# A fused two-block transformer kernel: order of the first weight load, low half, operand halves and copies

## The chip, the cores and the metric

The kernel runs on one core of one Trainium2 chip. The metric is the device time of one execution in microseconds. It computes in fp32 accuracy by splitting each operand of a matrix product into a high half, rounded to the format fp32r, and a low half, the remainder.

## The reference

The reference is a chain of three transformer layers on 256 tokens of width 1024: a first block with two layers, conditioned on a vector `c`, and a second block with one. The change touches only the start of the first layer:

```python
cond = jax.nn.silu(c)
mod = (cond @ ada_w[i] + ada_b[i])[:, None, :]
shift1, scale1, gate1, shift2, scale2, gate2 = jnp.split(mod, 6, axis=-1)
h = rmsnorm(x, norm1_g[i]) * (1.0 + scale1) + shift1
qkv = h @ w_qkv            # 1024 x 3072 in the first layer
```

So the product with `w_qkv` can't begin before `cond @ ada_w` is known for shift and scale, which are 2048 columns of 1024 rows, 8 MB. The rest of the kernel is attention, the feed-forward parts and the second block, in the same manner of computing.

## The kernel before

The program is written for each engine by hand; engines wait on each other's semaphores (`wait_ge`), and each engine and each queue works in program order.

*Weights.* All weights pass in tiles of 512 KB, numbered through the whole kernel. SyncE loads tile m to one of 4 buffers `raw`, after `low(m - 4)` has freed it (`slot_free`). ScalarE makes the high half `w_hi` (`split(m)`, line 638), VectorE the low half `w_lo` (`low(m)`, line 1156), which raises `lo_done`. TensorE waits for `lo_done` m + 1 and does 12 matmuls of 512 columns (`wide`, lines 1900 to 1902): for two token halves and two rows of blocks, high x high, high x low, low x high. There are 6 buffers of `w_hi` and `w_lo`, and a split waits for the tile 6 ahead of it to be done (`SPL`). Tiles 0 to 23 are the QKV projection (`TILES_A` orders them as column chunk and quarter u of the contraction: tiles 0 to 5 take quarters 0 and 1, tiles 6 to 11 quarters 2 and 3).

*Modulation.* `ada_w` comes in pieces of 512 KB too (`load_ada(a)`), all on SyncE's queue: c, pieces 0 and 1, x, pieces 2 to 8, weight tiles 0 to 3, pieces 9 to 13, then tiles and pieces by turns. VectorE multiplies each by its element of `cond` and adds it up (`fold(a)`, line 1186, the first of a sum at line 1183). Eight folds make a vector, spread over 128 partitions; 16 pieces make two vectors, half 0 and half 1 of shift and scale together. `reduce_vector` on TensorE adds over the partitions by 16 one-column matmuls (line 2025): the first before tile 0, the second behind tile 4, and it waits for `fold(15)`. Then `modulate(h)` on VectorE makes `mod` and `gains` for its half, and for its two quarters kk the modulated operand: VectorE writes `hf_mod` (line 1339) from the normed and transposed x (`hf`), ScalarE writes the high half `h_hi` directly from `hf` (`high_0`, line 770, two instructions a quarter), and VectorE subtracts, which gives `h_lo` (line 1344) and raises `h_lo_ok`. Each tile waits for its quarter's `h_lo_ok`, quarter u as `h_lo_ok` u + 1.

*Order on VectorE:* folds 0 to 8, modulation of half 0 with `low(0)` inside it, behind its first `h_lo`; `low(1)`, `low(2)`, folds 9 and 10, `low(3)`, folds 11 and 12, `low(4)`, folds 13 to 15, `low(5)`, `low(6)` (written `low(SPL)`), modulation of half 1, and from then on a low half and now and then a fold (`low(QKV_A + SPL + m)`), with tables for the attention between them. *Order on ScalarE:* `split(0)`, `high_0` of quarters 0 and 1, splits 1 to 7, `high_0` of quarters 2 and 3, then split 8 and so on with the evacuation of finished chunks between. Attention scores begin behind tile 20.

Of the kernel before, what the change touches and what calls it, by code (L numbers as in the profile page):

```python
# [11 lines left out]
ALU = mybir.AluOpType  # L12
ACT = mybir.ActivationFunctionType
AX = mybir.AxisListType

P = 128
D = 1024
S = 256
T = S // P
# [16 lines left out]
QKV_A, WO_A, IN_0, OUT_0, QKV_B, WO_B, IN_1, OUT_1 = 0, 24, 32, 76, 98, 110, 118, 162  # L36
# [9 lines left out]
TILES_A = [(c, u) for u0 in (0, 2) for c in range(3) for u in (u0, u0 + 1)] + [(c, u) for c in range(3, 6) for u in range(4)]  # L46
BANKS_A = (0, 1, 2, 1, 0, 1)
# [90 lines left out]
def program(nc, x_in, c_in, ada_w, ada_b, norm1_g, norm2_g, a_w_qkv, a_w_o, lq1, lk1, lq2, lk2,  # L138
# [4 lines left out]
    with ctx:  # L143
        def sem(name):
            return ctx.enter_context(nc.semaphore(name))
# [7 lines left out]
        w_hi = sb("w_hi", [P, SPL, 2, CH], F32R)  # L153
        w_lo = sb("w_lo", [P, SPL, 2, CH], F32R)
        h_hi = sb("h_hi", [P, KD, S], F32R)
        h_lo = sb("h_lo", [P, KD, S], F32R)
# [6 lines left out]
        mod = sb("mod", [P, 8 * VECTORS])  # L163
        gains = sb("gains", [P, KD])
# [48 lines left out]
        hf = at_p("hf", [P, KD, S], 2048)  # L213
        hf_mod = at_p("hf_mod", [P, KD // 2, S], 4096)
# [28 lines left out]
        bank = [ctx.enter_context(nc.psum_tensor(f"bank{n}", [P, CH], F32)) for n in range(8)]  # L243
# [14 lines left out]
        lo_done = sem("lo_done")  # L258
        mm_done = sem("mm_done")
# [22 lines left out]
        raw_x = sem("raw_x")  # L282
        hf_ok = sem("hf_ok")
        h_hi_ok, h_lo_ok = sem("h_hi_ok"), sem("h_lo_ok")
        res_ok = sem("res_ok")
        x_ok = sem("x_ok")
        evac = sem("evac")
        gate_mm, gate_ok = sem("gate_mm"), sem("gate_ok")
        bias_zero, bias_in = sem("bias_zero"), sem("bias_in")
        s_act = sem("s_act")  # L290
# [49 lines left out]
        def _(sp):  # L340
# [50 lines left out]
                load_ada(a)  # L391
            for t in range(T):
                sp.dma_start(x[:, t], x_in[0, t * P:(t + 1) * P, :]).then_inc(x_load, 16)
            for a in range(2, 9):
                load_ada(a)
            for m in range(4):
                load_a(m)
            for a in range(9, 14):
                load_ada(a)
# [23 lines left out]
            for k in range(KF):  # L423
                if k + 8 < KF:
                    load_tall(OUT_0 + 8 + k, f_w_out[0], 8 + k)
                else:
                    m = k + 8 - KF
# [201 lines left out]
        def _(act):  # L629
# [135 lines left out]
            def high_0(kk):  # L765

                act.wait_ge(raw_x, kk + 1)
                act.wait_ge(gain_ok, kk // 2 + 1)
                for k in (2 * kk, 2 * kk + 1):
                    last = nc.scalar.activation(h_hi[:, k], hf[:, k], ACT.Identity, scale=gains[:, k:k + 1],  # L770
                                                bias=mod[:, k:k + 1])
                last.then_inc(h_hi_ok, 1)

            act.wait_ge(setup_t, 2)
            nc.scalar.activation(vecs[:], bank[1][:, 0:237], ACT.Copy).then_inc(setup, 1)
# [54 lines left out]
            for i in range(NH + 3):  # L830
                if 2 <= i < NH:
                    exp_a(i)
                if 2 <= i < NH + 2:
                    h = i - 2
# [7 lines left out]
                if i >= 3:  # L842
                    h = i - 3
# [153 lines left out]
            for t in range(T):  # L997
                last = nc.scalar.activation(proj[:, t, 0:1536], proj[:, t, 0:1536], ACT.Gelu)
# [3 lines left out]
            for t in range(T):  # L1002
                last = nc.scalar.activation(rope_tc[:].rearrange("p a b c -> p (a b c)"), proj[:, t, 768:1536], ACT.Square,
                                            accum_out=stat[:, SS + t:SS + t + 1])
# [135 lines left out]
        def _(v_):  # L1140
# [9 lines left out]
            def low(m, turn=None):  # L1150

                if m >= END:
                    return
                m = at(m, turn, LOOP)
                v_.wait_ge(hi_done, m + 1)
                ve.tensor_tensor(w_lo[:, m % SPL], raw[:, m % RAW], w_hi[:, m % SPL].bitcast(F32),  # L1156
                                 ALU.subtract).then_inc(lo_done, 1)
                if m in TAKE_AFTER:
                    take_vector(TAKE_AFTER[m])
                for a, q in FOLD_AFTER.items():  # L1160
                    if q == m:
                        fold(a)

            def fold(a):

                g, k = divmod(a, 8)
                tile, arrived, count = ada_tile(a)
                acc, w = acc_of(g), tile.rearrange("p a n -> p (a n)")
                v_.wait_ge(arrived, count)
                if k == 0:  # L1170
                    if g in SHARED_WITH:

                        v_.wait_ge(ada_red, COLUMN[SHARED_WITH[g]] + 1)
                    if g:

                        v_.wait_ge(ada_done, a)
                    if g in GATES:

                        v_.wait_ge(bias_in, 16 * (GATES.index(g) + 1))
                        ve.scalar_tensor_tensor(out=acc, in0=w, scalar=cond[:, 0:1], in1=acc, op0=ALU.mult,  # L1180
                                                op1=ALU.add).then_inc(ada_done, 1)
                    else:
                        ve.tensor_scalar(acc, w, cond[:, 0:1], None, ALU.mult).then_inc(ada_done, 1)
                else:
                    v_.wait_ge(ada_done, a)
                    last = ve.scalar_tensor_tensor(out=acc, in0=w, scalar=cond[:, k:k + 1], in1=acc, op0=ALU.mult, op1=ALU.add)  # L1186
                    if k < 7 or g not in BY_BLOCKS:
                        last.then_inc(ada_done, 1)
                    else:

                        link(last)
                        link(ve.transpose(w, acc))
                        v_.wait_ge(ada_red, COLUMN[g])
                        ve.tensor_reduce(block_sums[:], w.rearrange("p (b r) -> p b r", r=32), AX.X, ALU.add).then_inc(ada_done, 1)
# [130 lines left out]
            def modulate(h):  # L1325

                v_.wait_ge(ada_red, h + 1)
                part = lambda row, first: row[:, first:first + 16].rearrange("p (v h q) -> p h v q", v=2, h=2)[:, h]
                ve.tensor_tensor(part(mod, 0), sums_of(h).rearrange("p (v q) -> p v q", v=2), part(vecs, ADAB_V),
                                 ALU.add).then_inc(ada_col, 1)  # L1330
                v_.wait_ge(ada_col, h + 1)
                ve.scalar_tensor_tensor(out=gains[:, 4 * h:4 * h + 4], in0=mod[:, 8 + 4 * h:12 + 4 * h], scalar=1.0,
                                        in1=vecs[:, N1_V + 4 * h:N1_V + 4 * h + 4], op0=ALU.add,
                                        op1=ALU.mult).then_inc(gain_ok, 1)
                v_.wait_ge(gain_ok, h + 1)
                for kk in (2 * h, 2 * h + 1):
                    v_.wait_ge(raw_x, kk + 1)
                    for k in (2 * kk, 2 * kk + 1):
                        last = ve.tensor_scalar(hf_mod[:, k % 4], hf[:, k], gains[:, k:k + 1], mod[:, k:k + 1],
                                                ALU.mult, ALU.add)  # L1340
                    last.then_inc(hf_ok, 1)
                    v_.wait_ge(hf_ok, kk + 1)
                    v_.wait_ge(h_hi_ok, kk + 1)
                    ve.tensor_tensor(h_lo[:, 2 * kk:2 * kk + 2], hf_mod[:, 2 * kk % 4:2 * kk % 4 + 2],
                                     h_hi[:, 2 * kk:2 * kk + 2].bitcast(F32), ALU.subtract).then_inc(h_lo_ok, 1)
                    if kk == 0:
                        low(0)

            for a in range(8):
                fold(a)  # L1350
            fold(8)
            v_.wait_ge(setup, 2)
            modulate(0)
            low(1)
            low(2)
            fold(9)
# [5 lines left out]
            for a in range(13, 16):  # L1362
                fold(a)
            low(5)
            low(SPL)
            modulate(1)

            def minus_lambda():
                v_.wait_ge(side_in, 16 * SIDE)
# [513 lines left out]
        def _(pe):  # L1883
            mm = nc.tensor.matmul

            def wide(m, u, b, v, turn=None, wait_operand=False, wait_1=None):


                if wait_operand:
                    pe.wait_ge(h_lo_ok, 4 * OLD[v] + u + 1)  # L1890
                m = at(m, turn, LOOP)
                pe.wait_ge(lo_done, m + 1)
                s = m % SPL
                for t in range(T):
                    if t == 1 and wait_1 is not None:
                        pe.wait_ge(*wait_1)
                    o = bank[2 * b + t][:]
                    for k in range(2):
                        hi, lo = (h[:, 2 * u + k, t * P:(t + 1) * P] for h in (h_hi, h_lo))
                        mm(o, hi, w_hi[:, s, k], start=(u == 0 and k == 0), stop=False)  # L1900
                        mm(o, hi, w_lo[:, s, k], start=False, stop=False)  # L1901
                        last = mm(o, lo, w_hi[:, s, k], start=False, stop=(u == 3 and k == 1))  # L1902
                last.then_inc(mm_done, 1)
# [143 lines left out]
            nc.tensor.transpose(bank[1][:, ADAB_V:ADAB_V + 96], stage_v[0:96, 2, :], ident[0:96, 0:96]).then_inc(setup_t, 1)  # L2047
            reduce_vector(0)

            def tile_a(m):  # L2050

                c, u = TILES_A[m]
                wide(QKV_A + m, u, BANKS_A[c], 0, wait_operand=True)

            for m in range(8):
                if m == 4:
# [510 lines left out]
```

## Time and profile before

| | us |
|---|---|
| median of 3 runs | 1038.45 (1038.05 to 1038.98) |
| span of the profiled execution | 1033.8 |
| median less that span | 4.65 |

The page's first table, as busy time and share of the span: TensorE (PE) 986.3 us, 95%; VectorE (DVE) 740.2 us, 72%; ScalarE (ACT) 542.6 us, 52%; GpSimd (POOL) 68.4 us, 7%. The profiled execution has its own span and no separate time outside it is recorded, so its place against the median is the difference above. In the page's 40 slices of 25.8 us the first has TensorE at two tenths, and the granted clock is nine tenths or more everywhere but in that slice, where it is eight. Queues: the core's 16 DMA engines moved 219.89 MB, 213 GB/s over the span. A matmul's row gives its start and its duration; matmuls overlap, so it is their distance that counts. A row of another engine may carry in brackets how long the engine was idle before and what ended the wait.

### The profile page before, as it was taken

To read this page: it belongs to the slowest core of one execution; us is meant where nothing else is said; L and a number is where in the kernel's file an instruction comes from. 1 tells how busy PE (TensorE), PEld (TensorE's weight loads), DVE (VectorE), ACT (ScalarE), POOL (GpSimd) and SP (SyncE) were. 2 spreads that over 40 slices of the span, in tenths; PEclk is the share of its full clock that TensorE was granted. 3 is DMA by queue.
4 is the path that set the end of the run, shared out by engine and by line. 5 is a ranking of instruction groups with operands and counts; after the bars stand their busy time and mean duration, and the time that the engine had idled before them with its cause. 6 is when DMAs were issued, how large, how long until landed. Compare 5 with 4: busy or idle time off the path is not lost.

```text
span 1033.8 us, 13550 instructions
## 1 busy us (share of the span) xinstructions
PE 986.3 (95%) x5102; PEld 827.2 (80%) x5102; DVE 740.2 (72%) x1053; ACT 542.6 (52%) x875; POOL 68.4 (7%) x126
## 2 busy tenths in 40 slices
PE   2999799999999999999999999999999999999997
PEld 2887577888878787778888886888888779999986
DVE  5988888878877897887665447647753777777643
ACT  4466846544443485575444436575546474444442
POOL 2100222000000411010000002000000010000000
PEclk8999999999999999999999999999999999999999
DMA  9998167998889472449865553856444367656551
GB/s 339 371 371 285 39 204 230 344 321 295 273 304 359 162 250 101 143 127 321 263 203 186 183 184 108 269 160 205 134 142 143 119 190 218 187 177 189 184 184 41
DMA packets 126968, 219.89 MB, mean 213 GB/s; under 512 B 9235, under 2 KB 78088, under 8 KB 126904
## 3 DMA queue, kind: packets, MB, share of 16 engines
q1 hardware_dynamic: 125200, 215.52, 63.4%
q0 software_dynamic: 1088, 2.87, 0.8%
q8 instruction: 40, 0.66, 0.3%
q10 hardware_dynamic: 616, 0.65, 0.2%
q14 instruction: 24, 0.20, 0.1%
HBM read 217.96 MB, written 1.05 MB: 212 GB/s over the span
## 4 chain that ended last, share of the span: by engine, by line
PE 84%; DVE 8%; ACT 4%; issue 2%; DMA 1%; POOL 0%; SPq 0%; POOLq 0%; DVEq 0%; ACTq 0%
PE bank L1900 13%; PE bank L1902 13%; PE bank L1901 13%; PE bank L1913 5%; PE bank L1915 5%; PE bank L1914 5%; PE bank L2504 3%; PE bank L2505 3%; PE bank L2506 3%; DVE w_lo L1156 2%; PE bank L1961 2%; PE bank L1963 2%; PE bank L1962 2%; ACT w_hi L638 1%; DVE ada_acc L1186 1%
## 5 line engine op out<-in xcount | busy, mean ns | idle before, releaser
L1156 DVE TENSOR_TENSOR w_lo<-raw,w_hi 128x1024 fp32r<-128x1024 f32 x312 | 379.1, 1223 | 215.3 <-ACT w_hi L638 214.5
L638 ACT ACTIVATE w_hi<-raw 128x1024 fp32r<-128x1024 f32 x312 | 328.2, 1061 | 338.4 <-PE bank L1902 139.7
L1900 PE MATMUL bank<-w_hi,h_hi 128*128 128x512 f32 x608 | 244.3, 402 | 3.7 <-DVE w_lo L1156 3.7
L1902 PE MATMUL bank<-w_hi,h_lo 128*128 128x512 f32 x608 | 238.3, 392 | 0.0
L1901 PE MATMUL bank<-w_lo,h_hi 128*128 128x512 f32 x608 | 237.9, 391 | 0.0
L1900 PEld LDWEIGHTS bank<-w_hi,h_hi 128*128 128x128 f32 x608 | 114.8, 189 | 28.4 <-issue 6.1
L1902 PEld LDWEIGHTS bank<-w_hi,h_lo 128*128 128x128 f32 x608 | 114.7, 189 | 24.6
L1901 PEld LDWEIGHTS bank<-w_lo,h_hi 128*128 128x128 f32 x608 | 114.9, 189 | 23.6 <-issue 1.0
L2504 PE MATMUL bank<-h_hi,w_hi 128*128 128x256 f32 x320 | 90.8, 284 | 1.1 <-DVE conv_t L1828 1.1
L2505 PE MATMUL bank<-h_hi,w_lo 128*128 128x256 f32 x320 | 90.7, 283 | 0.0
L2506 PE MATMUL bank<-h_lo,w_hi 128*128 128x256 f32 x320 | 90.7, 283 | 0.0
L1913 PE MATMUL bank<-w_hi,u_hi 128*128 128x512 f32 x200 | 78.5, 392 | 0.0
L1915 PE MATMUL bank<-w_hi,u_lo 128*128 128x512 f32 x200 | 77.9, 390 | 0.0
L1914 PE MATMUL bank<-w_lo,u_hi 128*128 128x512 f32 x200 | 77.9, 390 | 0.0
L2504 PEld LDWEIGHTS bank<-h_hi,w_hi 128*128 128x128 f32 x320 | 61.5, 192 | 1.4 <-DVE conv_t L1828 1.3
L2505 PEld LDWEIGHTS bank<-h_hi,w_lo 128*128 128x128 f32 x320 | 61.5, 192 | 0.0
L2506 PEld LDWEIGHTS bank<-h_lo,w_hi 128*128 128x128 f32 x320 | 61.5, 192 | 0.0
L1186 DVE SCALAR_TENSOR_TENSOR ada_acc<-ada,cond,ada_acc 128x1024 f32<-128x1024 f32 x38 | 48.6, 1280 | 4.4 <-DMA ada<-in_ada_w 3.9
L1914 PEld LDWEIGHTS bank<-w_lo,u_hi 128*128 128x128 f32 x200 | 37.6, 188 | 7.9 <-issue 0.2
L1913 PEld LDWEIGHTS bank<-w_hi,u_hi 128*128 128x128 f32 x200 | 37.6, 188 | 7.9 <-issue 0.2
L1915 PEld LDWEIGHTS bank<-w_hi,u_lo 128*128 128x128 f32 x200 | 37.5, 188 | 7.8
L1943 PE MATMUL bank<-w_hi,h_hi 128*128 128x512 f32 x80 | 33.0, 412 | 4.0 <-DVE h_lo L1284 2.4
(328 smaller groups left out, 1372.2 us busy)
## 6 DMA issues: line engine op xcount, KB each, us to landing
raw<-in_f_w_in SPq DMA_DIRECT2D x176, 256.0 KB
ada<-in_ada_w SPq DMA_DIRECT2D x86, 512.0 KB, 5.9
raw<-in_w_in SPq DMA_DIRECT2D x46, 512.0 KB
raw<-in_f_w_out SPq DMA_DIRECT2D x44, 512.0 KB
raw<-in_w_up SPq DMA_DIRECT2D x88, 256.0 KB
raw<-in_a_w_qkv SPq DMA_DIRECT2D x24, 512.0 KB
raw<-in_w_down SPq DMA_DIRECT2D x22, 512.0 KB
raw<-in_b_w_qkv SPq DMA_DIRECT2D x12, 512.0 KB
```

Of the source, the lines that this page charges most:

```text
L638: nc.scalar.activation(w_hi[:, m % SPL], raw[:, m % RAW], ACT.Copy).then_inc(hi_done, 1)
L1156: ve.tensor_tensor(w_lo[:, m % SPL], raw[:, m % RAW], w_hi[:, m % SPL].bitcast(F32), ALU.subtract).then_inc(lo_done, 1)
L1186: last = ve.scalar_tensor_tensor(out=acc, in0=w, scalar=cond[:, k:k + 1], in1=acc, op0=ALU.mult, op1=ALU.add)
L1900: mm(o, hi, w_hi[:, s, k], start=(u == 0 and k == 0), stop=False)
L1901: mm(o, hi, w_lo[:, s, k], start=False, stop=False)
L1902: last = mm(o, lo, w_hi[:, s, k], start=False, stop=(u == 3 and k == 1))
L1913: mm(o, hi, w_hi[:, s, n], start=first, stop=False)
L1914: mm(o, hi, w_lo[:, s, n], start=False, stop=False)
L1915: last = mm(o, lo, w_hi[:, s, n], start=False, stop=last_k)
L2504: mm(o, hi, h_hi[:, 2 * u + k], start=(u == 0 and k == 0), stop=False)
L2505: mm(o, lo, h_hi[:, 2 * u + k], start=False, stop=False)
L2506: last = mm(o, hi, h_lo[:, 2 * u + k], start=False, stop=(u == 3 and k == 1))
```

## The change

- SyncE: tile 0 is loaded ahead of piece 8 of `ada_w` instead of behind it.
- VectorE: `low(0)` comes behind fold 7 and ahead of the first modulation; `fold(8)` comes behind that modulation. `modulate(1)` comes ahead of `low(SPL)` instead of behind it, and for half 1 VectorE makes no `hf_mod` any more: it waits for a new semaphore `mod_a`, counted once a quarter.
- ScalarE: for quarters 2 and 3 it writes `hf_mod` too, two more instructions each, behind the quarter's `h_hi`, and raises `mod_a`.
- TensorE: tile 0 gets a function of its own, `first_tile`: eight matmuls with `h_hi` first, which wait for `h_hi_ok` and `lo_done`, and then the four with `h_lo`, behind the wait for `h_lo_ok`. Their sums go to the same banks.

```diff
--- before.py
+++ after.py
@@ -285,6 +285,7 @@
         res_ok = sem("res_ok")
         x_ok = sem("x_ok")
         evac = sem("evac")
+        mod_a = sem("mod_a")
         gate_mm, gate_ok = sem("gate_mm"), sem("gate_ok")
         bias_zero, bias_in = sem("bias_zero"), sem("bias_in")
         s_act = sem("s_act")
@@ -391,9 +392,11 @@
                 load_ada(a)
             for t in range(T):
                 sp.dma_start(x[:, t], x_in[0, t * P:(t + 1) * P, :]).then_inc(x_load, 16)
-            for a in range(2, 9):
+            for a in range(2, 8):
                 load_ada(a)
-            for m in range(4):
+            load_a(0)
+            load_ada(8)
+            for m in range(1, 4):
                 load_a(m)
             for a in range(9, 14):
                 load_ada(a)
@@ -770,6 +773,11 @@
                     last = nc.scalar.activation(h_hi[:, k], hf[:, k], ACT.Identity, scale=gains[:, k:k + 1],
                                                 bias=mod[:, k:k + 1])
                 last.then_inc(h_hi_ok, 1)
+                if kk >= 2:
+                    for k in (2 * kk, 2 * kk + 1):
+                        last = nc.scalar.activation(hf_mod[:, k % 4], hf[:, k], ACT.Identity, scale=gains[:, k:k + 1],
+                                                    bias=mod[:, k:k + 1])
+                    last.then_inc(mod_a, 1)
 
             act.wait_ge(setup_t, 2)
             nc.scalar.activation(vecs[:], bank[1][:, 0:237], ACT.Copy).then_inc(setup, 1)
@@ -1334,23 +1342,25 @@
                                         op1=ALU.mult).then_inc(gain_ok, 1)
                 v_.wait_ge(gain_ok, h + 1)
                 for kk in (2 * h, 2 * h + 1):
-                    v_.wait_ge(raw_x, kk + 1)
-                    for k in (2 * kk, 2 * kk + 1):
-                        last = ve.tensor_scalar(hf_mod[:, k % 4], hf[:, k], gains[:, k:k + 1], mod[:, k:k + 1],
-                                                ALU.mult, ALU.add)
-                    last.then_inc(hf_ok, 1)
-                    v_.wait_ge(hf_ok, kk + 1)
+                    if h == 0:
+                        v_.wait_ge(raw_x, kk + 1)
+                        for k in (2 * kk, 2 * kk + 1):
+                            last = ve.tensor_scalar(hf_mod[:, k], hf[:, k], gains[:, k:k + 1], mod[:, k:k + 1],
+                                                    ALU.mult, ALU.add)
+                        last.then_inc(hf_ok, 1)
+                        v_.wait_ge(hf_ok, kk + 1)
+                    else:
+                        v_.wait_ge(mod_a, kk - 1)
                     v_.wait_ge(h_hi_ok, kk + 1)
-                    ve.tensor_tensor(h_lo[:, 2 * kk:2 * kk + 2], hf_mod[:, 2 * kk % 4:2 * kk % 4 + 2],
+                    ve.tensor_tensor(h_lo[:, 2 * kk:2 * kk + 2], hf_mod[:, 2 * (kk % 2):2 * (kk % 2) + 2],
                                      h_hi[:, 2 * kk:2 * kk + 2].bitcast(F32), ALU.subtract).then_inc(h_lo_ok, 1)
-                    if kk == 0:
-                        low(0)
 
             for a in range(8):
                 fold(a)
-            fold(8)
+            low(0)
             v_.wait_ge(setup, 2)
             modulate(0)
+            fold(8)
             low(1)
             low(2)
             fold(9)
@@ -1362,8 +1372,8 @@
             for a in range(13, 16):
                 fold(a)
             low(5)
+            modulate(1)
             low(SPL)
-            modulate(1)
 
             def minus_lambda():
                 v_.wait_ge(side_in, 16 * SIDE)
@@ -2047,10 +2057,30 @@
             nc.tensor.transpose(bank[1][:, ADAB_V:ADAB_V + 96], stage_v[0:96, 2, :], ident[0:96, 0:96]).then_inc(setup_t, 1)
             reduce_vector(0)
 
+            def first_tile():
+
+                c, u = TILES_A[0]
+                pe.wait_ge(h_hi_ok, 1)
+                pe.wait_ge(lo_done, QKV_A + 1)
+                for t in range(T):
+                    for k in range(2):
+                        for w in (w_hi, w_lo):
+                            mm(bank[2 * BANKS_A[c] + t][:], h_hi[:, k, t * P:(t + 1) * P], w[:, QKV_A, k],
+                               start=(k == 0 and w is w_hi), stop=False)
+                pe.wait_ge(h_lo_ok, 1)
+                for t in range(T):
+                    for k in range(2):
+                        last = mm(bank[2 * BANKS_A[c] + t][:], h_lo[:, k, t * P:(t + 1) * P], w_hi[:, QKV_A, k],
+                                  start=False, stop=False)
+                last.then_inc(mm_done, 1)
+
             def tile_a(m):
 
                 c, u = TILES_A[m]
-                wide(QKV_A + m, u, BANKS_A[c], 0, wait_operand=True)
+                if m == 0:
+                    first_tile()
+                else:
+                    wide(QKV_A + m, u, BANKS_A[c], 0, wait_operand=True)
 
             for m in range(8):
                 if m == 4:
```

## Rows read from the trace of the kernel before

**Rows 1.** Busy time by stretch: bounds, length, PE, PEld, DVE, ACT, POOL, PEclk, DMA, GB/s.

```profile
65.70:91.40 25.70, 25.70 (x131) 21.14 (x129) 19.88 (x27) 14.61 (x21) 0.00 (x0) 1.00 0.89 312
```

**Rows 2.** TensorE's waits: 25.7 to 102 us, then whole span (us, times, longest).

```profile
PE bank L1900 <- DVE w_lo L1156: 3.7, 1, 3.7
...
PE bank L2134 <- ACT wgtT L836: 7.2, 5, 2.5
```

**Rows 3.** Chain of waits in order of time: start, us, what; before the first modulation.

```profile
19.25 2.72 PE bank L2025 x16
```

**Rows 4.** VectorE in order of time (start, us, line, tiles), first modulation.

```profile
19.30 0.75 DVE L1183 TENSOR_SCALAR gate_row<-early,cond 128x1024 f32<-128x1024 f32 x1
...
22.06 0.17 DVE L1329 TENSOR_TENSOR mod<-bank,vecs 128x8 f32<-128x8 f32 x1 [2.01 <-PE bank L2025]
...
23.72 0.69 DVE L1344 TENSOR_TENSOR h_lo<-hf_mod,h_hi 128x512 fp32r<-128x512 f32 x1 [0.36 <-ACT h_hi L770]
24.32 1.22 DVE L1156 TENSOR_TENSOR w_lo<-raw,w_hi 128x1024 fp32r<-128x1024 f32 x1
```

**Rows 5.** TensorE in order of time: tile 0, second reduction, tile 6, transposes after tile 7.

```profile
25.69 0.77 PE L1900 MATMUL bank<-w_hi,h_hi 128*128 128x512 f32 x1 [3.74 <-DVE w_lo L1156]
...
28.39 0.63 PE L1900 MATMUL bank<-w_hi,h_hi 128*128 128x512 f32 x1
28.82 0.63 PE L1901 MATMUL bank<-w_lo,h_hi 128*128 128x512 f32 x1
...
41.63 1.84 PE L2025 MATMUL bank<-ones,gate_row 128*128 128x1 f32 x16
...
46.19 0.39 PE L1900 MATMUL bank<-w_hi,h_hi 128*128 128x512 f32 x1
...
51.63 0.60 PE L2064 MATMUL bank<-ident,w_sp 128*128 128x128 f32 x4
```

**Rows 6.** VectorE in order of time, last folds and second modulation.

```profile
38.24 2.67 DVE L1186 SCALAR_TENSOR_TENSOR gate_row<-ada,cond,gate_row 128x1024 f32<-128x1024 f32 x2
40.84 2.35 DVE L1156 TENSOR_TENSOR w_lo<-raw,w_hi 128x1024 fp32r<-128x1024 f32 x2
43.51 0.17 DVE L1329 TENSOR_TENSOR mod<-bank,vecs 128x8 f32<-128x8 f32 x1 [0.32 <-PE bank L2025]
...
45.17 0.69 DVE L1344 TENSOR_TENSOR h_lo<-hf_mod,h_hi 128x512 fp32r<-128x512 f32 x1 [0.52 <-ACT h_hi L770]
45.77 0.73 DVE L1339 TENSOR_SCALAR hf_mod<-hf,gains,mod 128x256 f32<-128x256 f32 x2
46.58 0.69 DVE L1344 TENSOR_TENSOR h_lo<-hf_mod,h_hi 128x512 fp32r<-128x512 f32 x1
47.19 2.35 DVE L1156 TENSOR_TENSOR w_lo<-raw,w_hi 128x1024 fp32r<-128x1024 f32 x2
```

**Rows 7.** Busy time by stretch, columns as in rows 1: transfer rate and granted clock.

```profile
24.00:26.00 2.00, 0.31 (x1) 0.34 (x2) 2.00 (x4) 2.00 (x4) 0.00 (x0) 0.50 1.03 337
...
30.50:31.00 0.50, 0.50 (x4) 0.40 (x3) 0.40 (x2) 0.00 (x0) 0.00 (x0) 1.00 1.04 385
...
91.40:110.00 18.60, 16.09 (x93) 11.82 (x92) 16.74 (x31) 15.23 (x43) 0.00 (x0) 1.00 0.72 252
...
153.50:154.00 0.50, 0.50 (x3) 0.41 (x2) 0.47 (x4) 0.40 (x1) 0.00 (x0) 0.50 0.00 0
...
156.50:157.00 0.50, 0.50 (x3) 0.42 (x2) 0.10 (x1) 0.10 (x1) 0.37 (x1) 0.73 0.81 279
```

**Rows 8.** ScalarE in order of time; first, line 770's durations (ns, min/median/max).

```profile
L770 ACT ACTIVATE h_hi<-hf,mod,gains x8: 583/585/602, 22.5 to 45.5; 128x256 fp32r<-128x256 f32 x8
...
20.48 1.06 ACT L638 ACTIVATE w_hi<-raw 128x1024 fp32r<-128x1024 f32 x1 [3.13 <-DMA raw<-in_a_w_qkv]
...
43.97 2.08 ACT L770 ACTIVATE h_hi<-hf,mod,gains 128x256 fp32r<-128x256 f32 x4 [1.91 <-DVE gains L1332]
...
50.87 1.06 ACT L638 ACTIVATE w_hi<-raw 128x1024 fp32r<-128x1024 f32 x1 [1.53 <-DMA raw<-in_a_w_qkv]
```

**Rows 9.** SyncE's queue of transfers in order of time: the load of tile 10.

```profile
43.22 0.40 SPq L354 DMA_DIRECT2D raw<-in_a_w_qkv  x1
```

## The prediction, made before the changed kernel ran

> **What bounds the kernel now.** The change touches only the first 50 us of the span, so I asked first whether time won or lost there reaches the end. By the table of stretches, TensorE is busy for all of the 25.70 us from 65.70 [rows 1]. By the list of waits, between the first matmul of the QKV projection and 102 us it waits for another engine once, 3.7 us, at that first matmul [rows 2]. VectorE is busy for 19.88 us of the same 25.70 [rows 1], so it follows TensorE there. A microsecond by which TensorE is early or late once the tiles run without a gap is therefore a microsecond at the end of the projection, and what follows takes its start from there.
>
> Next, what sets the first matmul. The chain of waits runs through VectorE's folds of `ada_w` and then, from 19.25, the 16 one-column matmuls of the reduction [rows 3]. VectorE's order of time then goes `mod` at 22.06, `h_lo` at 23.72, `w_lo` of tile 0 at 24.32 [rows 4], and the first matmul starts 25.69 [rows 5]: 0.15 us after that `w_lo` ends (24.32 + 1.22 = 25.54).
>
> Last, the second modulation. Its reduction starts at 41.63 and tile 6 at 46.19 [rows 5]. TensorE has no wait there, but tile 6 needs `h_lo` of quarter 2 (done 45.17 + 0.69 = 45.86) and `low(6)`. Now `low(6)` stands in the pair at 40.84 [rows 6]: it is done at 43.19, while VectorE would otherwise wait for the reduction.
>
> **The change part by part.** *Load order.* One 512 KB transfer leaves the queue ahead of tile 0's weights. At the 385 GB/s of 30.50 to 31.00 it is 524,288 / 385,000 = 1.36 us; at the 337 GB/s of 24 to 26 us, 1.56 us [rows 7]. I take 1.36, since the queue is full at 20 us as well. The high half, which now starts at 20.48 when its load lands [rows 8], starts near 19.1 and ends near 20.2. `low(0)` then runs from 20.2 to 21.5, inside the wait for the reduction, which ends 22.06 [rows 4]. Cover left: 0.6 us. If the load were not sooner, `low(0)` would end at 20.48 + 1.06 + 0.1 + 1.22 = 22.9 and push the modulation by 0.8 us.
>
> *First tile.* It needs `h_hi` of quarter 0, ready 0.1 us before `h_lo` starts at 23.72 [rows 4], so it starts near 23.77 instead of 25.69: 1.92 us sooner. Eight of its matmuls use the high operand only; they are 0.43 us apart at the clock of 28 us and (51.63 - 46.19) / 24 = 0.227 at the full one [rows 5], so at least 1.8 us pass, so `h_lo` (24.41) is no wait.
>
> *What VectorE carries on with.* `low(0)`, 1.22 us, leaves the path between the modulation and the folds, and `fold(8)`, 0.75 us, comes in [rows 4]. All later work of VectorE up to `fold(15)` moves by 1.22 - 0.75 = 0.47 us only. The pair of folds that starts at 38.24 ends at 40.91 now [rows 6] and at 40.44 then. The second reduction stands behind tile 4 in TensorE's program, and needs that fold. TensorE, 1.9 us early, is stopped there: the reduction starts at 40.5 instead of 41.63, 1.1 us sooner. Of 1.92 us, 0.8 are gone. This hardly depends on when the clock rises: with the rise at 30.5, where it is now, 6.7 us pass at the low clock, in which 15.7 of the 60 matmuls of tiles 0 to 4 are done, and the other 44.3 x 0.227 = 10.1 us end at 40.5; with an earlier rise TensorE only waits longer for the fold.
>
> *Second modulation.* `mod` follows the reduction's start by 43.51 - 41.63 = 1.88 us, so it is at 42.4, and ScalarE starts 43.97 - 43.51 = 0.46 us later [rows 6, 8], at 42.85. It now has eight instructions: high half and modulated copy, for two quarters of two. Four take 2.08 us now [rows 8]: three pitches and one duration of 0.585. A pitch is 0.50, and eight take 7 x 0.50 + 0.585 = 4.07 us. The copy has the same shape and form as the high half; it writes fp32 instead of fp32r, which no row prices, and I take the same. The bounds for a copy are 0.37 us (VectorE's price for that shape, two in 0.73 [rows 6]), in all 4 x 0.13 = 0.5 us less, and the duration 0.585, in all 0.3 us more. `mod_a` reaches 2 at 46.9. VectorE, which saves four copies (1.5 us), waits for it: `h_lo` of quarter 3 starts at 47.0.
>
> *The order of `modulate(1)` and `low(SPL)`.* `low(6)` is now queued behind both waits on `mod_a`, and tile 6 waits for `lo_done` 7, which only `low(6)` gives. The pair of `h_lo` and `w_lo` is 47.19 - 46.58 = 0.61 us apart [rows 6], so `low(6)` starts at 47.6, ends at 47.6 + 1.22 = 48.85, and tile 6 starts 0.15 us later at 49.0. Tile 5 ends near 40.5 + (46.19 - 41.63) = 45.1. TensorE idles for 3.9 us where it had no gap. Tile 6 comes at 49.0 instead of 46.19: **2.8 us later**. The cost stands on one engine's order, not on a duration: even with copies for nothing, the four high halves alone take ScalarE to 44.9 and `low(6)` could not start before 45.6.
>
> *The queue behind it.* SyncE loads tile 10 after `low(6)`. That issue is at 43.22 now [rows 9] and its high half runs at 50.87 [rows 8], 7.65 us later. Issued at 48.9, by the same distance the high half is at 56.5 and the low half done by 59.0. Tile 10 starts no sooner than 49.0 + 4 x 2.72 = 59.9. It is hidden, with 0.9 us to spare, more as the queue is emptier. `low(7)`, next on VectorE, is done by 50.1, ahead of tile 7 at 51.7.
>
> Sum: -1.1 (reduction sooner) + 3.9 (gap) = +2.8 us on the profiled span of 1033.8, that is 1036.6. The median of the runs lies 4.65 above the span; the same distance gives 1038.45 + 2.8 = 1041.25.
>
> *A rule against the row.* The rows have ScalarE at 0.50 us in pitch for a 128x256 piece [rows 8] and VectorE at 0.37 [rows 6]. The Trainium skill, "ScalarE: Activation LUTs", section "Rules for kernel authors", says to put multiply and add on VectorE instead, where it is up to about three times faster in bf16; and it budgets about 0.3 us plus 0.83 ns an element, 0.51 us here. The trace agrees with the direction and the 0.51, not with a factor of three in fp32. By that budget the eight take 4.1 us and the sum is the same.
>
> **Rivals.** *R1, the gap drops the clock.* At 24 us, after the 16 one-column matmuls of the first reduction and an idle stretch, the granted clock stands at 0.50, and it is at 1.00 again at 30.5, 4.8 us after the first matmul; at 153.5 it stands at 0.50 once more and is on its way back between 156.5 and 157 [rows 7]. The longest of the attention's waits, 2.5 us [rows 2], left it at 1.00 through the stretch from 91.40 [rows 7]. The new gap is 3.9 us, longer than any that kept it, with a reduction 2.8 us ahead of it. If the clock falls to 1.2 GHz (half), the next tiles run at 0.43 instead of 0.227 us a matmul for 3.2 us (153.5 to 156.7) to 4.8: half of that is lost, 1.6 to 2.4 us. Time 1042.9 to 1043.7. The Trainium skill, "TensorE: Matmul & The Clock Gate", section "Why this matters for your kernels", says that an idle gap between bursts returns the engine to the lower clock; by that rule this rival holds. The 2.5 us gap neither supports nor refutes it. Chance 0.18.
>
> *R2, the load isn't sooner.* The transfers share 16 engines, and `low(0)` ends at 22.9. Everything from the modulation on is 0.8 us later, `fold(15)` included: +2.8 + 0.8, 1042.1. Against it: the landing at 20.48 fits a queue that lands one 1.36 us piece after another. Chance 0.05.
>
> *R3, VectorE is the bound, and the time falls.* If the end of the projection is set by VectorE's queue rather than TensorE's, then the four copies taken off it (1.5 us) and the 0.46 us count: 1038.45 - 2.0 = 1036.5. It decides if VectorE is without idle time before the scores at 91 us. Its 19.88 of 25.70 us [rows 1] speaks against it. Chance 0.04.
>
> *R4, later slack takes a part.* TensorE waits 7.2 us in the attention [rows 2], and if ScalarE or VectorE is ahead there, up to 2.3 us of the 2.8 come back: 1038.9 to 1040.5. Against it: each of these waits hangs on scores that TensorE itself gives out late. Chance 0.15.
>
> **How the numbers follow.** The forecast as told has the remaining 0.58, and with the bounds of the copies it lies between 1040.6 and 1042.0. The predicted time is 1041.3. The range reaches up over R2 and R1 and down into R4, 1039.7 to 1043.6; about 0.1 of R4 and R3 and a little above are left out. A measurement of this kernel can tell some 0.2% from no change, 2.1 us, so slower means above 1040.5. Forecast, R1, R2: 0.81, less 0.04 for a start that scatters with the clock: slower 0.77. R4 and that remainder: same 0.18. R3 and a little: faster 0.05.
>
> **What would show it.** First matmul near 23.8; second reduction near 40.5, released by `fold(15)`; a TensorE wait of some 3.9 us ended by `w_lo` at 49.0; ScalarE with eight pieces in 4.1 us; the granted clock behind the gap tells R1. The prediction is wrong if tile 6 starts before 47.5, or if it starts at 49 and the score stage does not come 2.8 us later.

## The result and the profile after

| | us |
|---|---|
| kernel before, median of 20 runs | 1038.87 (1036.45 to 1043.46) |
| changed kernel, median of 20 runs | 1043.88 (1040.60 to 1048.61) |
| ratio | 1.0049, 95% interval 1.0038 to 1.0060 |
| profiled execution after: span, own time | 1046.0, 1047.7 |

The change costs 5.0 us. The direction was forecast, the size was not: 1041.3 was predicted, and the range ended at 1043.6.

Two bookkeeping facts first. In the profiled executions that have a time of their own, it lies 1.7 to 2.0 us above the span. By that the profiled execution of before took some 1035.5 to 1035.8 us (an estimate, its own time is not on record), below all of its 20 runs. Of the 4.65 us that the prediction put between span and median, some 3 are then the luck of one execution. The profile after is a long one of its kernel. The difference of the spans, 12.2 us, is therefore not the effect.

The rows of the start can be read one by one against the prediction. VectorE in order of time, as in rows 4 and 6:

```profile
20.20 1.23 DVE L1164 TENSOR_TENSOR w_lo<-raw,w_hi 128x1024 fp32r<-128x1024 f32 x1 [0.90 <-ACT w_hi L641]
23.03 0.17 DVE L1337 TENSOR_TENSOR mod<-bank,vecs 128x8 f32<-128x8 f32 x1 [1.61 <-PE bank L2035]
...
38.88 2.67 DVE L1194 SCALAR_TENSOR_TENSOR gate_row<-ada,cond,gate_row 128x1024 f32<-128x1024 f32 x2
...
46.22 0.69 DVE L1355 TENSOR_TENSOR h_lo<-hf_mod,h_hi 128x512 fp32r<-128x512 f32 x1 [2.27 <-ACT hf_mod L778]
48.14 0.69 DVE L1355 TENSOR_TENSOR h_lo<-hf_mod,h_hi 128x512 fp32r<-128x512 f32 x1 [1.22 <-ACT hf_mod L778]
48.74 3.49 DVE L1164 TENSOR_TENSOR w_lo<-raw,w_hi 128x1024 fp32r<-128x1024 f32 x3
```

`low(0)` has moved ahead of the modulation and hides there. In the second modulation VectorE waits twice for ScalarE, 2.27 and 1.22 us, and `low(6)` is the first of the three that start at 48.74.

ScalarE in order of time, as in rows 8:

```profile
19.11 1.06 ACT L641 ACTIVATE w_hi<-raw 128x1024 fp32r<-128x1024 f32 x1 [1.57 <-DMA raw<-in_a_w_qkv]
...
44.05 1.10 ACT L773 ACTIVATE h_hi<-hf,mod,gains 128x256 fp32r<-128x256 f32 x2 [2.46 <-DVE gains L1340]
45.05 1.09 ACT L778 ACTIVATE hf_mod<-hf,mod,gains 128x256 f32<-128x256 f32 x2
46.04 1.08 ACT L773 ACTIVATE h_hi<-hf,mod,gains 128x256 fp32r<-128x256 f32 x2
47.02 1.08 ACT L778 ACTIVATE hf_mod<-hf,mod,gains 128x256 f32<-128x256 f32 x2
```

TensorE in order of time, as in rows 5:

```profile
19.35 3.57 PE L2035 MATMUL bank<-ones,ada_acc 128*128 128x1 f32 x16 [2.23 <-DVE ada_acc L1194]
24.64 0.80 PE L2068 MATMUL bank<-w_hi,h_hi 128*128 128x512 f32 x1 [1.72 <-ACT h_hi L773]
...
41.60 1.95 PE L2035 MATMUL bank<-ones,gate_row 128*128 128x1 f32 x16 [0.90 <-DVE gate_row L1194]
...
50.11 0.77 PE L1910 MATMUL bank<-w_hi,h_hi 128*128 128x512 f32 x1 [3.67 <-DVE w_lo L1164]
...
58.12 0.60 PE L2094 MATMUL bank<-ident,w_sp 128*128 128x128 f32 x4
```

Tile 6 waits 3.67 us for `w_lo`. The transposes behind tile 7 come at 58.12 instead of 51.63, 6.49 us late. That is worked out from these rows and rows 5: reduction to tile 6 takes 8.51 us instead of 4.56 (+3.95), tiles 6 and 7 take 8.01 instead of 5.44 (+2.57), and the reduction starts at the same time (-0.03). The 2.57 us are the clock; stretches with TensorE's busy time, granted clock, DMA share and GB/s:

```profile
44.00:46.00 2.00, 2.00 (x10) 1.00 0.99 348
46.00:48.00 2.00, 0.44 (x2) 1.00 0.79 313
48.00:50.00 2.00, 0.00 (x0) 0.64 0.02 8
50.00:52.00 2.00, 1.89 (x5) 0.50 0.45 72
52.00:54.00 2.00, 2.00 (x6) 0.50 1.00 395
54.00:56.00 2.00, 2.00 (x7) 0.66 1.03 401
```

It falls inside the gap and comes back at about 55.4.

What lies between 58 and the end (12.2 - 6.5 = 5.7 us) comes in steps, by the distance of the same TensorE rows in both traces. Half of it is the clock again: 1.4 us behind a wait in the attention, where it stands at 0.50 between 114 and 116, and 1.5 us between 488.8 and 492.4, at 0.50 too and behind a wait of 1.90 us for `act_u` that the kernel before doesn't have there. The rest is that wait, 0.5 us by 191 and smaller pieces. The attention's wait is the same in both kernels and the clock behind it is not. Before, where the clock stays at 1.00, and after:

```profile
107.39 0.63 PE L2134 MATMUL bank<-ident,wgt 128*128 128x128 f32 x4 [2.49 <-ACT wgtT L836]
```

```profile
113.88 1.09 PE L2164 MATMUL bank<-ident,wgt 128*128 128x128 f32 x4 [2.49 <-ACT wgtT L844]
```

Stretches after, with TensorE's busy time, granted clock, DMA share and GB/s:

```profile
112.00:114.00 2.00, 0.12 (x1) 0.85 0.38 154
114.00:116.00 2.00, 2.00 (x10) 0.50 0.00 0
116.00:118.00 2.00, 2.00 (x14) 0.80 0.00 0
```

The second profile of the changed kernel (E9 below) has neither of these falls, +3.86 us at the transposes and +4.1 at the end. The second profile of the kernel before (E0) starts like the first and is 4.0 us later by its end, with a wait of 2.74 us and a clock of 0.50 behind it at 868 to 870. So these steps are scatter that both kernels have.

### The profile page after: what moved, and what is told of

It is laid out like the page before. It is cut to its first block, busy times and chain, and to the rows that moved or that the text cites. A ratio compares the mean times of both kernels' runs of the same rounds, so it can differ in the third digit from the quotient of the medians.

```text
span 1046.0 us, 13549 instructions
## 1 busy us (share of the span) xinstructions
PE 993.1 (95%) x5102; PEld 831.3 (79%) x5102; DVE 739.1 (71%) x1049; ACT 545.1 (52%) x879; POOL 68.6 (7%) x126
## 4 chain that ended last, share of the span: by engine, by line
PE 78%; DVE 11%; ACT 4%; DMA 3%; issue 3%; SPq 1%; POOL 0%; POOLq 0%; DVEq 0%; ACTq 0%
PE bank L1910 12%; PE bank L1912 12%; PE bank L1911 12%; PE bank L1923 5%; PE bank L1925 5%; PE bank L1924 5%; PE bank L2534 3%; PE bank L2535 3%; PE bank L2536 3%; DVE w_lo L1164 3%; PE bank L1971 2%; PE bank L1973 2%; PE bank L1972 2%; ACT w_hi L641 1%; DMA raw<-in_f_w_in 1%
```

## The experiments

All ratios are against the kernel before, measured beside the experiment. "Transposes" is the start of the transposes behind tile 7 in the profile; reduction is the start of the second reduction. Their distance leaves out how early or late an execution arrived there.

| kernel | ratio (95% interval) | median, us | reduction | transposes | distance | clock falls on the way |
|---|---|---|---|---|---|---|
| before, E0 | | | 41.63, 41.44 | 51.63, 51.44 | 10.00, 10.00 | no, no |
| changed | 1.0049 (1.0038 to 1.0060) | 1043.88 | 41.60 | 58.12 | 16.52 | in the gap |
| E9 changed again | 1.0041 (1.0026 to 1.0056) | 1044.07 | 41.45 | 55.49 | 14.04 | in tile 5, 1.3 us behind the reduction |
| E1 order back | 1.0014 (1.0000 to 1.0027) | 1039.80 | 41.23 | 52.93 | 11.70 | at the reduction |
| E2 order only | 1.0030 (1.0013 to 1.0046) | 1042.17 | 41.59 | 54.01 | 12.42 | no |
| E3 copies on VectorE | 1.0019 (1.0005 to 1.0033) | 1040.82 | 41.37 | 54.71 | 13.34 | at the reduction |
| E4 start only | 1.0020 (1.0005 to 1.0036) | 1040.86 | | | | |
| E4b start only again | 1.0000 (0.9979 to 1.0021) | 1039.75 | 41.33 | 54.60 | 13.27 | at the reduction |
| E5 gap filled | 1.0039 (1.0022 to 1.0056) | 1043.78 | 41.60 | 56.48 | 14.88 | at the reduction |
| E6 start, reduction filled | 0.9989 (0.9970 to 1.0008) | 1038.30 | 40.93 | 50.97 | 10.04 | no |
| E6b the same again | 0.9996 (0.9979 to 1.0014) | 1039.08 | 42.15 | 52.19 | 10.04 | no |
| E7 copies only | 1.0026 (1.0011 to 1.0041) | 1042.35 | 42.90 | 54.12 | 11.22 | no |
| E8 both filled | 1.0029 (1.0014 to 1.0044) | 1042.41 | 42.30 | 56.29 | 13.99 | no |

**E1, the order undone.**

```diff
             low(5)
-            modulate(1)
             low(SPL)
+            modulate(1)
```

> The changed kernel with low(6) ahead of the second modulation again; everything else of the change stays. Theory T1, the place of low(6) makes the loss: the gap of 3.7 us ahead of tile 6 goes; tile 6 starts some 5.4 us after the second reduction starts (ScalarE's first two pairs), tile 7 some 8.5 us after it, so tile 7 is 1.3 us later than it could be but no gap is longer than 1.5 us and the clock stays at 1.00. Time near the kernel before, +0.7 us (0 to +1.5). Theory T2, the copies on ScalarE make it: still +3 to +5 us. Theory T3, the load order or the first tile makes it: still +4 to +5 us.

1.0014: most of the loss goes with this swap, as T1 has it; T2 and T3 as sole causes fall. But the profile has the clock at 0.50 from 43.3 to 46.7, where TensorE has no idle time any more. That was in no theory. The columns are as above:

```profile
41.00:43.00 2.00, 1.77 (x16) 1.00 0.79 244
43.00:44.00 1.00, 1.00 (x5) 0.66 1.05 390
44.00:46.00 2.00, 2.00 (x6) 0.50 1.02 373
```

**E2, the order alone, in the kernel before.**

```diff
             low(5)
-            low(SPL)
             modulate(1)
+            low(SPL)
```

> The kernel before with one thing changed: low(6) behind the second modulation, whose copies stay on VectorE. T1: tile 6 starts at reduction + 6.9 us instead of + 4.6, a gap of 2.3 us on TensorE, time +2.3 us, more in an execution in which the clock falls in that gap. T2 and T3: no change, within 0.5 us.

Tile 6 in order of time on TensorE:

```profile
41.59 1.84 PE L2025 MATMUL bank<-ones,gate_row 128*128 128x1 f32 x16
...
48.48 0.47 PE L1900 MATMUL bank<-w_hi,h_hi 128*128 128x512 f32 x1 [2.17 <-DVE w_lo L1156]
```

48.48 - 41.59 = 6.89 us (6.9 expected), transposes 2.4 us late, ratio 1.0030: 3.1 us, with 2.3 inside the interval. This one swap of two lines makes a loss by itself. The clock stays at 1.00 in its profile, behind an idle gap of 2.17 us.

**E3, the copies back on VectorE, order as changed.** The diff takes the two activations behind `h_hi` out and lets `modulate(1)` make `hf_mod` as `modulate(0)` does.

```diff
-                if kk >= 2:
-                    for k in (2 * kk, 2 * kk + 1):
-                        last = nc.scalar.activation(hf_mod[:, k % 4], hf[:, k], ACT.Identity, scale=gains[:, k:k + 1],
-                                                    bias=mod[:, k:k + 1])
-                    last.then_inc(mod_a, 1)
```

> The changed kernel with the second modulation's copies on VectorE again, low(6) still behind it. T1: tile 6 at reduction + 6.9 us instead of + 8.5, so 1.6 us of the loss goes, and with the gap at 2.4 instead of 3.7 us the clock falls less often: +1 to +3 us against the kernel before. T2: the loss is gone, -1 to 0 us. T3: still +4 to +5 us.

+2.0 us, as T1 has it. Its profile shows no wait of TensorE ahead of tile 6: tile 5 and the reduction ran at the low clock, and so TensorE was late itself.

**E4 and E4b, the start alone.** Both edits above taken back; load order, `low(0)` and `first_tile` stay.

> The changed kernel with both the order and the copies as before: only the load order, low(0) ahead of the modulation and the first tile with its high half first. T1 and T2: the first matmul 1.9 us sooner, the second reduction 0.5 to 1.1 us sooner (then fold 15 is late), no gap ahead of tile 6: -0.5 to -1.1 us against the kernel before. T3: +3 us or more.

> The start alone again (load order, low(0) ahead of the modulation, first tile with its high half first; order and copies of the second modulation as before). The first time it came out 0.2% above the kernel before, in runs that scattered. Theory C: the early start only leads to a wait of some 0.5 to 0.9 us for fold 15, and that wait and the 16 one-column matmuls of the second reduction make the granted clock fall to 0.50 in most executions, which costs 1.5 to 2 us on tiles 5 and 6: +0.5 to +1.5 us against the kernel before, with the clock at 0.50 near 43 to 46 us in the profile. Theory T1 as first told, without the clock: -0.5 to -1.1 us, clock at 1.00 there.

1.0020 and 1.0000: the gain I expected is in neither. The profiled execution of E4 was disturbed as a whole (a span of 3558 us) and is not used; one more of its twelve took 1419.8 us, and its median is that of the other ten. The profile of E4b shows where a gain can go. TensorE in order of time:

```profile
41.33 2.32 PE L2027 MATMUL bank<-ones,gate_row 128*128 128x1 f32 x16 [0.86 <-DVE gate_row L1188]
43.51 0.77 PE L1902 MATMUL bank<-w_hi,h_hi 128*128 128x512 f32 x1
44.08 0.63 PE L1903 MATMUL bank<-w_lo,h_hi 128*128 128x512 f32 x1
44.51 0.63 PE L1904 MATMUL bank<-w_hi,h_lo 128*128 128x512 f32 x1
```

And its stretch behind the reduction, with TensorE's busy time, granted clock, DMA share and GB/s:

```profile
43.00:44.00 1.00, 1.00 (x5) 0.50 1.03 381
```

TensorE arrives 0.86 us before `fold(15)` is ready. After this wait and the 16 one-column matmuls the granted clock is 0.50 up to 49.6, and the tiles' matmuls stand 0.43 us apart. The distance to the transposes is 13.27 instead of 10.00 us. That is one execution: the medians of E4b and of the kernel before are equal to 0.2 us, so a loss of 3 us isn't that of most of them. The kernel before goes through the same reduction without a wait and keeps its clock, in both profiles.

**E6 and E6b, that wait filled.** The start alone, and five matmuls whose sums nobody reads ahead of the reduction.

```diff
                 if m == 4:
+                    for n in range(5):
+                        mm(bank[7][:], h_hi[:, 0, 0:P], h_hi[:, 0:2].rearrange("p k s -> p (k s)"), start=True, stop=True)
                     reduce_vector(1)
```

> The start alone, plus five matmuls of 512 columns between tile 4 and the second reduction, whose sums nobody reads (1.1 us of TensorE's time, which it would wait for fold 15). Theory C: the clock stays at 1.00 through the reduction and the gain of the start shows: -0.5 to -1.1 us against the kernel before, 1 to 2 us below the start alone. If the clock at the reduction is not the cause: no better than the start alone, or up to 0.5 us worse.

> The start alone with five matmuls ahead of the second reduction, again, for a narrower interval. The trace of the first one has the transposes after tile 7 0.7 us sooner than the kernel before, so theory C gives -0.7 us (-1.1 to -0.3); if the gain does not reach the end: within 0.3 us of the kernel before.

```profile
39.79 1.30 PE L2083 MATMUL bank<-h_hi 128*128 128x512 f32 x5
40.93 1.87 PE L2027 MATMUL bank<-ones,gate_row 128*128 128x1 f32 x16
...
50.97 0.60 PE L2088 MATMUL bank<-ident,w_sp 128*128 128x128 f32 x4
```

The clock holds in both profiles, the distance is 10.04 us, and in E6 the transposes are 0.7 us sooner than in the first profile of before (0.5 than in E0). So the start does not need to cost the clock: with matmuls in place of the wait it held in two of two profiles, where it had fallen in E4b. The medians point the same way, -0.11% and -0.04%, but neither interval excludes no change. This is the best version found; that it beats the kernel before is not shown. In E6b the first reduction started at 19.72 instead of 19.28 and took 3.57 us instead of 2.92, and the transposes came at 52.19, 0.6 us later than before.

**E5, the gap ahead of tile 6 filled, in the changed kernel.** 14 matmuls of the same form behind tile 5 (`if m == 6:` ahead of `tile_a(m)`).

> The changed kernel whole, plus 14 matmuls of 512 columns between tiles 5 and 6 (3.2 us), whose sums nobody reads. The wait for low(6) is the same, tile 6 starts at the same distance from the reduction. If the fall of the clock in the gap makes the part of the loss beyond 2.8 us: +2.8 to +3.5 us against the kernel before, 1.5 to 2.5 below the changed kernel, clock 1.00 behind the gap. If the gap alone makes the loss: the time of the changed kernel, within 0.5 us.

1.0039, no better than the changed kernel by its interval. In its profile the clock falls at the reduction, not in the gap, so filling one of the two places is not enough to tell. The filling also costs here: tile 5 ran late at the low clock, the 14 matmuls began at 47.85 and tile 6 at 51.04, 9.44 us behind the reduction instead of 8.5, though `low(6)` was done at 50.2.

**E8, both places filled.** E5's 14 and E6's five.

> The changed kernel whole, with the idle time of TensorE filled at both places: five matmuls of 512 columns ahead of the second reduction and 14 between tiles 5 and 6, whose sums nobody reads. If the sum of the prediction was right but for the clock: transposes after tile 7 at 54.4 us (+2.8 us against 51.6), granted clock at 1.00 from 31 us on, and +2.8 us against the kernel before (2.3 to 3.5), 1.5 to 2.5 us below the changed kernel. If the clock has no part in the loss: the time of the changed kernel, +4.5 us or more.

```profile
41.16 1.30 PE L2094 MATMUL bank<-h_hi 128*128 128x512 f32 x5
42.30 1.87 PE L2035 MATMUL bank<-ones,gate_row 128*128 128x1 f32 x16
46.84 3.33 PE L2090 MATMUL bank<-h_hi 128*128 128x512 f32 x14
50.72 0.47 PE L1910 MATMUL bank<-w_hi,h_hi 128*128 128x512 f32 x1 [0.54 <-DVE w_lo L1164]
56.29 0.60 PE L2099 MATMUL bank<-ident,w_sp 128*128 128x128 f32 x4
```

The clock holds throughout. The distance is 13.99 us; the prediction's numbers give 49.0 - 40.5 + 5.44 = 13.9. The ratio is 1.0029, +3.0 us, against +2.8 predicted. The absolute 54.4 was missed: this execution came to its second reduction late, at 42.30, since its first started at 19.91 and took 3.58 us. Against the changed kernel beside it, 1042.41 against 1044.07, the intervals overlap, so the times alone do not show a part of the clock. More is in the granted clock of each run, which is on record for every execution and not only for the profiled one, as a mean over its span. The twelve of E9 average 0.9894 and the twelve of E8 0.9941, 0.0047 apart (0.0022 to 0.0071 by resampling); the 35 of the kernel before beside them average 0.9917. So the changed kernel does run more often or longer at the low clock when the two places are not filled. What that costs is less sure, since a low clock costs nothing while TensorE is idle.

**E7, the copies alone, in the kernel before.**

```diff
+                if kk >= 2:
+                    for k in (2 * kk, 2 * kk + 1):
+                        last = nc.scalar.activation(hf_mod[:, k % 4], hf[:, k], ACT.Identity, scale=gains[:, k:k + 1],
+                                                    bias=mod[:, k:k + 1])
+                    last.then_inc(mod_a, 1)
```

> The kernel before with one thing changed: the second modulation's copies on ScalarE (low(6) still ahead of it, load order and first tile as before). If the copies cost only by the two quarters coming later: h_lo of quarter 2 ends at reduction + 5.2 us, tile 6 follows at once, 0.7 us late, h_lo of quarter 3 ends at + 7.2, low(7) at + 8.4 and tile 7 starts there, 1.3 us late in all; +1.3 us, transposes after tile 7 at 52.9 instead of 51.6. If the copies are the main cost of the change: +3 us or more. If ScalarE has room for them: 0.

Distance 11.22 us, 1.2 more than before, as expected from the two quarters coming later. The ratio of 1.0026 is 2.7 us, more than that, with 1.3 us inside the interval. In its profile the transposes are 2.5 us late, the other 1.3 us since the second reduction came at 42.90; its first one took 3.57 us.

**E9 and E0, both kernels once more.**

> The changed kernel once more, beside the other three on one chip. From its own measurement: +0.4 to +0.6% against the kernel before, +4 to +6 us. Its profile tells whether the clock falls again in the gap ahead of tile 6 (theory R1: half of the executions or more), or, where it does not, at the second reduction: in either case some 8 to 12 matmuls of tiles 5 to 7 at 0.43 us.

> The kernel before once more, for a second profile of it. It had one fall of the granted clock after the projection (150 to 160 us) and none at its second reduction. If the clock's falls at the second reduction belong to the early start (theory C), this profile has none there either: TensorE comes to the reduction from matmuls, without a wait. If they fall at random, it may have one.

TensorE in E9:

```profile
41.45 1.95 PE L2035 MATMUL bank<-ones,gate_row 128*128 128x1 f32 x16 [0.88 <-DVE gate_row L1194]
49.93 0.47 PE L1910 MATMUL bank<-w_hi,h_hi 128*128 128x512 f32 x1 [2.48 <-DVE w_lo L1164]
```

Here the clock fell in tile 5, 1.3 us behind the reduction (0.69 in 44 to 46, 0.50 in 46 to 48) and was back at 1.00 before tile 6; tile 5 ran longer into the gap, so that the gap absorbed the low stretch: tile 6 is 8.48 us behind the reduction, as if nothing had happened, and the distance to the transposes is that of E8, 14.04 against 13.99. In the first profile the fall came inside the gap and hit tiles 6 and 7. Which of the two happens made +3.9 or +6.5 us at the transposes, and the +5.0 us of the medians lie between. How often each happens two profiles can't tell, and the profiled execution of E9 is the shortest of its twelve.

## Why the prediction was off

*What bounds the kernel* held: whatever delay the transposes behind tile 7 have stands unchanged at the scores (+6.49 in the changed kernel at both, +2.4 in E2).

*The start.* Load sooner and `low(0)` hidden: right (19.11, 20.20). First matmul predicted near 23.8, measured 24.64. The term that failed is the first reduction, taken as ending where it ended before: it took 3.57 us instead of 2.70, so all behind it came 1 us later. The change isn't needed for that: E7, whose start is that of before, shows 3.57 as well. But the other three profiles with the old start have 2.70, 2.12 (E0) and 2.78 (E2), and of the nine with the new start eight have 3.40 to 3.58 and one 2.92 (E6). Whether the change makes the slow one likelier stays open.

*TensorE stopped at the second reduction by `fold(15)`*: right, with a wait of 0.90 us. The start of the reduction, predicted at 40.5, was 41.60, by the same 1 us, and 41.45 in E9: of the term of -1.1 us in the sum, 0.0 to 0.2 came. E6, with a first reduction of 2.92 us, has 40.93. What I left out is what this wait does: I named the fold as the thing that is late next, and didn't ask whether idle time right ahead of a reduction of one-column matmuls costs the clock. In the profile of E4b the clock fell behind it, and a reduction 0.3 us sooner ended in transposes 3.0 us later.

*Eight pieces on ScalarE in 4.07 us*: 44.05 to 48.10, 4.05.

*The order of `modulate(1)` and `low(SPL)`*: tile 6 predicted 8.5 us behind the reduction, measured 8.51, 8.48 and, with all idle time filled, 8.42. The gap was 3.67 us against 3.9. The queue behind it stayed hidden: TensorE has no other wait before the attention.

*The sum.* Two of its steps failed. The first is the term "reduction sooner", -1.1 us, of which the two profiles of the changed kernel show 0.0 and 0.2; with the gap's +3.9 us as predicted that makes +3.9 us at the transposes, as in E9. The second is the clock, which the sum put at nothing and R1 at a chance of 0.18, for the gap alone and with no run that spoke for that number. In each of the three profiles of the changed kernel in which the reduction was not filled (the first, E9, E5), the clock fell at one of two places, and it cost 2.57 us in the first and nothing at the transposes in E9. With both places filled E8 measured +3.0 us (1.5 to 4.6), which agrees with the +2.8 of the sum, but is too wide to part the two steps: how the 2.2 us between the forecast change and the measured one divide between them stays open.

The prediction had one row on a wait of nearly that length, and rightly said that it neither supports nor refutes R1. The 2.49 us wait in the attention kept the clock at 1.00 in the trace of before, but that was one draw. The same wait stands in all 13 profiles, and in seven of them (changed, E1, E3, E4b, E6b, E7, E8) a stretch of 0.50 follows at or right behind it, in six (before, E0, E2, E5, E6, E9) none does. Read over more traces it would have spoken for a higher chance than 0.18.

R1's own time, 1042.9 to 1043.7, is 0.2 us short of the median of 1043.88. That is luck in part, since it stands on the sum whose reduction term was off by 1 us. Its price per fall was near: 2.57 us measured in the first profile, 1.6 to 2.4 forecast. Of the range, only the top was short, since it took R1 alone and left no room for the scatter of the baseline (20 runs of before gave 1038.87, three gave 1038.45).

*The conversion from span to median* went through a difference of 4.65 us that mixes the 1.7 to 2.0 us between span and time with the luck of one profile. It cancelled here, because only the change was added to the median.

R2 and R3 did not occur: the load of tile 0 was sooner (19.11), and the time rose. R4, later slack, did not either: nothing was given back after the transposes.

## What to carry to other kernels

When an operation is queued behind a new wait, look first at who waits for it: here a loss of 2.4 us in the trace of E2 came from swapping two lines, with no copy moved. Work won ahead of a join is worth only what the join's other arm allows, and the rest turns into idle time; if that idle time stands beside small matmuls, price the clock too, and don't take one profile in which a gap left the clock alone as proof that it will. Judge an effect of a few us by distances between marks in the trace and by many runs, never by the difference of two spans: one kernel's spans differed by 8 us.

## What the runs showed of the hardware

At the second reduction, TensorE's granted clock fell in or up to 1.3 us behind the 16 one-column matmuls in five of the six profiles in which 0.5 to 0.9 us of idle time stood ahead of them (E1, E3, E4b, E5, E9). In the sixth, the first profile of the changed kernel, with 0.90 us, it held until the gap. It fell in none of the seven in which matmuls of 512 columns stood directly ahead of the same reduction (before, E0, E2, E6, E6b, E7, E8). The Trainium skill, "TensorE: Matmul & The Clock Gate", section "Why this matters for your kernels", advises against idle gaps of more than some 3 us between bursts of matmuls. These traces agree with the direction and not with 3 us as a safe length: the gap of 3.67 us saw the clock fall inside it, the 0.5 to 0.9 us with small matmuls behind them were followed by a fall in five of six, the 2.49 us of the attention in seven of 13, and the 2.17 us of E2 in none.

The recorded clock can't be trusted at the start of a trace. In the profile of the changed kernel the stretch from 26 to 27 us reads 1.00 while its matmuls stand 0.43 us apart, the distance that goes with 0.50 elsewhere. Stretch with busy times by engine, clock, DMA share and GB/s:

```profile
26.00:27.00 1.00, 1.00 (x4) 0.73 (x3) 0.97 (x2) 1.00 (x2) 0.64 (x1) 1.00 1.05 389
```

TensorE in order of time there:

```profile
26.09 0.63 PE L2068 MATMUL bank<-w_lo,h_hi 128*128 128x512 f32 x1
26.51 0.63 PE L2068 MATMUL bank<-w_hi,h_hi 128*128 128x512 f32 x1
```

One-column matmuls too go at about half the pace at the low clock. The 16 of the first reduction took 3.40 to 3.58 us in nine of the 13 profiles and 2.12 to 2.92 in the other four, and the 16 of the second, with the clock recorded at 1.00 throughout, 1.84 to 1.95. That is 1.4 us of scatter on the path to the first tile, more than the 1.1 us that the sum gave the start of this change.
